# A two-block transformer kernel: the condition's broadcast loaded by stride-zero transfers, two small sums and one turn placed earlier

## The chip, the cores and the metric

The kernel runs on one core of a Trainium2 chip. A core has TensorE (PE, matrix products, with its weight loads shown as PEld), VectorE (DVE), ScalarE (ACT), GpSimd (POOL) and SyncE (SP), which here only issues transfers. The engines run their own instruction queues in order and wait for one another through semaphores. The metric is the device time of one execution in microseconds (us), lower is better. The time of a kernel is the median of its runs.

## The reference

A transformer block with two token streams (512 tokens of x, 256 of ctx, width 1024) is followed by a second block. What matters here stands at the start of the first: a condition vector c makes shifts, scales and gates for x (`adaln_params`), another, c_ctx, makes them for ctx; both streams are normed, modulated and projected by `w_in`. Lambda is one scalar of the attention.

```python
def rmsnorm(x, g):
    xf = x.astype(jnp.float32)
    y = xf * lax.rsqrt(jnp.mean(xf * xf, axis=-1, keepdims=True) + EPS)
    return (y * g.astype(jnp.float32)).astype(x.dtype)

def modulate(x, g, shift, scale):
    return rmsnorm(x, g) * (1 + scale) + shift

def adaln_params(cond, w_mod, b_mod):
    return jnp.split(jax.nn.silu(cond) @ w_mod + b_mod, 6, axis=-1)
...
        lam = (jnp.exp(jnp.sum(diff_lambda_q[l, 0] * diff_lambda_k[l, 0]))
               - jnp.exp(jnp.sum(diff_lambda_q[l, 1] * diff_lambda_k[l, 1])) + lam_init)
        sh1, sc1, gt1, sh2, sc2, gt2 = [m[:, None, :] for m in adaln_params(c, w_mod[l], b_mod[l])]
        csh1, csc1, cgt1, csh2, csc2, cgt2 = adaln_params(c_ctx, w_mod[l], b_mod[l])
        pc = project(modulate(ctx, norm1_g[l], csh1, csc1), w_in[l])
...
        px = project(modulate(x, norm1_g[l], sh1, sc1), w_in[l])
...
        x = x + gt1 * mix
        x = x + gt2 * swiglu(modulate(x, norm2_g[l], sh2, sc2), w_ffn_in[l], w_ffn_out[l])
```

All arithmetic is float32. The second block (pooling, attention, memory attention, a convolved feed-forward) is untouched.

## The kernel before

Activations lie with the 1024 features on the partitions, as eight tiles (k = 0 to 7) of 128 x 512 for x and 128 x 256 for ctx. A product with weights is made of three passes: each operand is split into a high part (`whi`, `hxh`, `hch`) and a rest (`wlo`, `hxl`, `hcl`), and TensorE adds high by high, high by rest and rest by high. Weights come in units of up to 128 x 1024 (`raw`, ring of four, loaded by SyncE in the order of a plan); ScalarE's `hi(upto)` makes `whi` (ring of three), `lo(upto)` on VectorE makes `wlo` (for units 1 and 2 GpSimd does). SyncE loads unit j when the rest of unit j - 4 has been made. Every engine's code is one hand-written sequence; there is no scheduler, and the order on an engine is the order of the lines.

The start of the program runs so:

- Transfers. ScalarE issues c and c_ctx as two rows (`crow`), `ident` and `vec`. SyncE issues, in this order on one queue, the modulation weights `mod1` pieces 0 to 3 (0.5 MB each), ctx (`cmT`), x (`xT`), pieces 4 to 15 with `raw` units 0 to 3 between and behind them, the constants, and `raw` 4 and on.
- TensorE turns the condition into columns (L2159), which ScalarE passes through Silu (`small`, semaphore `cb`). Then two products of a row of ones with a row of c (L2177, one partition deep) spread c over 128 partitions in banks 6 and 7, from where ScalarE's Silu puts it into `cbx` (L605).
- `mod_piece(n)` (L2188) multiplies the two condition columns with piece n: four matmul records each, pieces 0 to 7 for the first half of the features and 8 to 15 for the second. ScalarE copies the two result rows of a half out (`mod_rows`, `mrow`), `turn_mods(half)` (L2166) turns them back into columns, VectorE's `first_mods` adds the bias and makes the gains.
- `first_sums` (L2173) sums squares over the partitions for ctx (bank 4) and x (bank 5): ScalarE squares, VectorE adds, TensorE multiplies with ones. `root` on ScalarE and `newton` on VectorE make the reciprocal root. A like product of two columns makes the sums of lambda in bank 3 (L2201), of which ScalarE takes the exponential (L622) inside its loop over the split (i = 6).
- The loop i = 0 to 15 makes the normed tiles, x and ctx in turn: `first_norm` on VectorE (L1298), the high part on ScalarE (L629), `first_rest` on VectorE (L1305). i = 8 to 15 need the second half of the modulations.
- TensorE's first projection, "gqk", has eight steps k (L2238 to L2240 for x, into banks 0 to 3; L2246 to L2248 for ctx, into banks 4 and 5), 18 products each. Pieces 12 to 15 stand between steps 1 and 2, `turn_mods(1)` after step 2. A bank is written only when the semaphores in `freed[b]` have been reached; `fill(b)` waits for them.

The gates and the second pair of shift and scale need the rest of `w_mod`. They are not made on TensorE: its rows are loaded transposed (`mraw`), and `dots2` on VectorE multiplies each with the spread condition and sums, with `cbx` for rows 0 to 15 and `cbx2` from row 16. `cbx2` is made anew since its place is used by others between: ScalarE loads c again (`crow2`, L872) during the attention, TensorE spreads it by two one-row products into banks 4 and 5 (L2483) ahead of the output projection "wo", ScalarE applies Silu (L903). In "wo" each of the eight units m has 24 products (L2112 to L2114).

## Time and profile before

| | |
|---|---|
| median of three runs | 1660.71 us (1660.3 to 1662.28) |
| the profiled execution | 1659.81 us, its span 1658.2 us |
| TensorE busy | 1582.9 us, 95% of the span |
| VectorE busy | 938.3 us, 57% |
| ScalarE busy | 730.5 us, 44% |
| GpSimd busy | 125.1 us, 8% |
| transfers | 156.60 MB, mean 94 GB/s |

The profile is of one execution. "Busy" counts instructions that run; matmuls are pipelined, so a start and a length may overlap with the next. In a timeline a row has its start, its length and, in brackets, how long the engine stood idle before it and what released it; the first rows of the program lie within the first 75 us. Starts are counted from the span's start.

### The profile page before, as it was taken

How to read it: one execution, taken by the hardware profiler on the slowest of the kernel's cores; microseconds unless marked ns; L12 is line 12 of the kernel's file. 1: busy time of each engine (PE TensorE's matmuls, PEld its weight loads, DVE VectorE, ACT ScalarE, POOL GpSimd, SP SyncE). 2: the span in 40 equal slices, each digit the busy share in tenths (PEclk: the TensorE clock that was granted, in tenths of full speed). 3: DMA queues.
4: the chain of work that ended last, by engine and by line, in shares of the span. 5: the costliest groups of instructions: out<-in, count | busy, mean ns of one | idle time of the engine just before them, and what ended most of it. 6: DMA issues, size and time to landing. Idle time of an engine off the chain costs nothing.

```text
span 1658.2 us, 19178 instructions
## 1 busy us (share of the span) xinstructions
PE 1582.9 (95%) x7606; PEld 1245.1 (75%) x7606; DVE 938.3 (57%) x1441; ACT 730.5 (44%) x1130; POOL 125.1 (8%) x89
## 2 busy tenths in 40 slices
PE   7999999899899999999999899999987999999999
PEld 2677876677688888888878677788665788888885
DVE  4476787885844433334555555366656586257743
ACT  4344445675332222323342767455455444234432
POOL 0000123531000000000010011130010000000000
PEclk9999999699999999999999999999988999999999
DMA  9351111101534233222332222143202232333221
GB/s 376 130 188 52 50 50 54 64 1 66 176 114 147 75 108 106 100 78 88 102 102 70 63 69 74 44 142 106 78 24 91 64 115 70 108 114 92 83 89 54
DMA packets 47950, 156.60 MB, mean 94 GB/s; under 512 B 5587, under 2 KB 10323, under 8 KB 47350
## 3 DMA queue, kind: packets, MB, share of 16 engines
q1 hardware_dynamic: 47280, 152.00, 27.8%
q10 hardware_dynamic: 582, 3.38, 0.6%
q8 instruction: 61, 1.00, 0.2%
q14 instruction: 27, 0.22, 0.0%
HBM read 153.26 MB, written 2.10 MB: 94 GB/s over the span
## 4 chain that ended last, share of the span: by engine, by line
PE 79%; DVE 11%; ACT 6%; issue 3%; DMA 0%; POOL 0%; ACTq 0%; DVEq 0%
PE pall L2112 19%; PE pall L2113 18%; PE pall L2114 18%; PE pall L2605 2%; PE pall L2188 1%; PE pall L2130 1%; PE pall L2132 1%; PE pall L2131 1%; PE pall L2148 1%; PE pall L2607 1%; PE pall L2606 1%; PE pall L2149 1%; PE pall L2150 1%; DVE wlo L1243 1%; ACT whi L563 1%
## 5 line engine op out<-in xcount | busy, mean ns | idle before, releaser
L1243 DVE TENSOR_TENSOR wlo<-raw,whi 128x1024 fp32r<-128x1024 f32 (+2 forms) x261 | 290.6, 1115 | 313.5 <-ACT whi L563 313.3
L563 ACT ACTIVATE whi<-raw 128x1024 fp32r<-128x1024 f32 (+2 forms) x263 | 247.0, 941 | 208.9 <-PE pall L2114 177.3
L2112 PE MATMUL pall<-h5h,whi 128*128 128x512 f32 x320 | 125.8, 393 | 2.5 <-DVE wlo L1243 2.5
L2113 PE MATMUL pall<-h5l,whi 128*128 128x512 f32 x320 | 125.3, 392 | 0.0
L2114 PE MATMUL pall<-h5h,wlo 128*128 128x512 f32 x320 | 125.2, 391 | 0.0
L2112 PE MATMUL pall<-h2h,whi 128*128 128x512 f32 x320 | 124.6, 389 | 0.0
L2114 PE MATMUL pall<-h2h,wlo 128*128 128x512 f32 x320 | 124.6, 389 | 0.0
L2113 PE MATMUL pall<-h2l,whi 128*128 128x512 f32 x320 | 124.6, 389 | 0.0
L2112 PEld LDWEIGHTS pall<-h5h,whi 128*128 128x128 f32 x320 | 60.4, 189 | 15.7 <-issue 3.1
L2114 PEld LDWEIGHTS pall<-h5h,wlo 128*128 128x128 f32 x320 | 60.5, 189 | 12.7
L2113 PEld LDWEIGHTS pall<-h5l,whi 128*128 128x128 f32 x320 | 60.5, 189 | 12.6 <-issue 0.2
L2112 PEld LDWEIGHTS pall<-h2h,whi 128*128 128x128 f32 x320 | 60.1, 188 | 12.5
L2114 PEld LDWEIGHTS pall<-h2h,wlo 128*128 128x128 f32 x320 | 60.1, 188 | 12.5
L2113 PEld LDWEIGHTS pall<-h2l,whi 128*128 128x128 f32 x320 | 60.1, 188 | 12.3
L2113 PE MATMUL pall<-cl,whi 128*128 128x512 f32 x176 | 68.6, 390 | 0.0
L2114 PE MATMUL pall<-ch,wlo 128*128 128x512 f32 x176 | 68.6, 390 | 0.0
L2112 PE MATMUL pall<-fh,whi 128*128 128x512 f32 x176 | 68.5, 389 | 0.0
L2112 PE MATMUL pall<-ch,whi 128*128 128x512 f32 x176 | 68.5, 389 | 0.0
L2113 PE MATMUL pall<-fl,whi 128*128 128x512 f32 x176 | 68.5, 389 | 0.0
L2114 PE MATMUL pall<-fh,wlo 128*128 128x512 f32 x176 | 68.5, 389 | 0.0
L945 ACT ACTIVATE fh<-tmp 128x512 fp32r<-128x512 f32 x22 | 13.9, 632 | 95.1 <-DVE tmp L1695 95.1
L1912 DVE TENSOR_TENSOR pall<-pall,R 128x512 f32<-128x512 f32 x48 | 33.1, 695 | 35.2 <-PE pall L2114 31.2
(459 smaller groups left out, 3653.7 us busy)
## 6 DMA issues: line engine op xcount, KB each, us to landing
raw<-in_weights SPq DMA_DIRECT2D x204, 512.0 KB, 3.5
mraw<-in_wmod SPq DMA_DIRECT2D x32, 512.0 KB, 5.1
mod<-in_weights SPq DMA_DIRECT2D x16, 512.0 KB, 15.2
raw<-in_weights SPq DMA_DIRECT2D x25, 256.0 KB, 2.6
raw<-in_weights SPq DMA_DIRECT2D x32, 192.0 KB, 2.3
xT<-in_x SPq DMA_DIRECT2D x1, 2048.0 KB, 13.1
xT<-in_x ACTq DMA_DIRECT2D x1, 2048.0 KB, 8.2
out_y<-xT SPq DMA_DIRECT2D x8, 256.0 KB, 2.1
```

The source lines that it names most:

```text
L563: e.activation(whi[j % 3][:, 0:cols(j)], raw[j % 4][:, 0:cols(j)], ACT.Copy).then_inc(s.hi, 1)
L1243: e.tensor_tensor(wlo[j % 3][:, 0:n], raw[j % 4][:, 0:n], f(whi[j % 3][:, 0:n]), ALU.subtract).then_inc(s.lo_v, 1)
L1912: e.tensor_tensor(bank(b), bank(b), r, ALU.mult).then_inc(s.rq, 1)
L2112: e.matmul(o_, a[:, kk, :], xh(k), start=(k == 0), stop=False)
L2113: e.matmul(o_, a[:, kk, :], xl(k), start=False, stop=False)
L2114: mm = e.matmul(o_, b[:, kk, :], xh(k), start=False, stop=(k == nk - 1))
L2130: e.matmul(bank(o_), a[:, k % 2, c], xh(k), start=(k == 0), stop=False)
L2131: e.matmul(bank(o_), a[:, k % 2, c], xl(k), start=False, stop=False)
L2132: mm = e.matmul(bank(o_), b[:, k % 2, c], xh(k), start=False, stop=(k == 7))
L2148: e.matmul(bank(o_), h_, a[:, kk, :], start=(k + kk == 0), stop=False)
L2149: e.matmul(bank(o_), h_, b[:, kk, :], start=False, stop=False)
L2605: e.matmul(bank(b), a[:, k, :], xh[:, k, :], start=(k == 0), stop=False)
```

## The change

1. `cbx` is no longer made by products of one row: SyncE loads c into all 128 partitions by one transfer whose source has a stride of zero (128 x 1024 values, 0.5 MB written), after `raw` 3 and before the constants. ScalarE applies Silu in place, one instruction of 128 x 1024, at i = 8 of its split loop ahead of `mod_rows(1)`; this needs the Silu table and then the exponential's again.
2. `cbx2` is loaded in the same way by ScalarE's queue at n = 19 of the attention loop; `crow2` and the products of L2483 go.
3. The context sum stands after piece 3 instead of 5, lambda's sums behind it instead of after piece 11, the token sum after piece 7 instead of behind the first turn. Lambda's exponential stands behind the context root. On ScalarE `root("x")` stands before `hi(0)`.
4. `lo(0)` on VectorE stands inside the loop, behind the first `first_rest`.
5. `turn_mods(1)` stands inside step 2, after two of its four x groups.

The diff, with its declarations left out:

```diff
@@ SyncE
             for j in range(2, 4):
                 load(j)
+            e.dma_start(cbx[:, :], ap["cc"][:, 0, :].to_broadcast([128, 1024])).then_inc(s.cc, 16)
             for dst, name in consts:
@@ ScalarE
-            for j in range(2):
-                w.wait_ge(s.p_cb, 2 + j)
-                e.activation(cbx[:, 512 * j:512 * j + 512], bank(6 + j), ACT.Silu).then_inc(s.cb, 1)
             for q in range(16):
...
             root("ctx", bank(4, 256), 256, D)
+            w.wait_ge(s.lam_p, 1)
+            e.activation(small[:, 4:6], bank(3, 2), ACT.Exp).then_inc(s.lam_a, 1)
             mod_rows(0)
+            root("x", bank(5), 512, D)
             hi(0)
-            root("x", bank(5), 512, D)
             for i in range(16):
-                if i == 6:
-                    w.wait_ge(s.lam_p, 1)
-                    e.activation(small[:, 4:6], bank(3, 2), ACT.Exp).then_inc(s.lam_a, 1)
                 if i == 8:
+                    w.wait_ge(s.cc, 48)
+                    e.activation(cbx[:, :], cbx[:, :], ACT.Silu).then_inc(s.cb, 1)
+                    table[0] = "silu"
+                    use_exp()
                     mod_rows(1)
...
-                if n == 5:
-                    e.dma_start(crow2[0:1, :], ap["cc"][:, 0, :]).then_inc(s.cc, 16)
+                if n == 19:
+                    e.dma_start(cbx2[:, :], ap["cc"][:, 0, :].to_broadcast([128, 1024])).then_inc(s.cc, 16)
...
             w.wait_ge(s.kql, 8)
-            for j in range(2):
-                w.wait_ge(s.p_cb, 4 + j)
-                e.activation(cbx2[:, 512 * j:512 * j + 512], bank(4 + j), ACT.Silu).then_inc(s.cb, 1)
+            w.wait_ge(s.cc, 64)
+            e.activation(cbx2[:, :], cbx2[:, :], ACT.Silu).then_inc(s.cb, 1)
             table[0] = "silu"
             use_exp()
@@ VectorE
             first_mods(0)
-            lo(0)
             newton("x", bank(5), 512, D)
             for i in range(16):
...
                 if i and i != 8:
                     first_rest(i - 1)
+                if i == 1:
+                    lo(0)
@@ TensorE
-            w.wait_ge(s.g_const, 2)
-            for j in range(2):
-                e.matmul(bank(6 + j), ones[0:1, :], crow[0:1, 512 * j:512 * j + 512], start=True, stop=True).then_inc(s.p_cb, 1)
-                freed[6 + j] = [(s.cb, 2 + j)]
             w.wait_ge(s.cb, 1)
...
             for n in range(9):
                 mod_piece(n)
-                if n == 5:
+                if n == 3:
                     first_sums(4, 256, 7, acc_c)
+                    w.wait_ge(s.lam_v, 1)
+                    fill(3)
+                    e.matmul(bank(3, 2), ones[:, :], small[:, 2:4], start=True, stop=True).then_inc(s.lam_p, 1)
+                    freed[3] = [(s.lam_a, 1)]
+                if n == 7:
+                    first_sums(5, 512, 14, acc)
             turn_mods(0)
-            first_sums(5, 512, 14, acc)
             for n in range(9, 12):
                 mod_piece(n)
-            w.wait_ge(s.lam_v, 1)
-            fill(3)
-            e.matmul(bank(3, 2), ones[:, :], small[:, 2:4], start=True, stop=True).then_inc(s.lam_p, 1)
-            freed[3] = [(s.lam_a, 1)]
...
                 for i in range(4):
+                    if k == 2 and i == 2:
+                        turn_mods(1)
+                        freed[6] = [(s.mdv, 4)]
+                        freed[7] = [(s.mdr, 4)]
...
-                if k == 2:
-                    turn_mods(1)
-                    freed[6] = [(s.mdv, 4)]
-                    freed[7] = [(s.mdr, 4)]
...
-            w.wait_ge(s.cc, 48)
-            for j in range(2):
-                fill(4 + j)
-                e.matmul(bank(4 + j), ones[0:1, :], crow2[0:1, 512 * j:512 * j + 512], start=True, stop=True).then_inc(s.p_cb, 1)
-                freed[4 + j] = [(s.cb, 4 + j)]
```

TensorE before, between piece 5 and the first step (`acc_c` and `acc` are the summed squares of ctx and x, `small` the columns of lambda, `mrow` the rows that are turned):

```order
L2188 MATMUL pall<-mod_5,small 2x512 x2
L2173 MATMUL pall<-acc_c,ones 128x256
L2188 MATMUL pall<-mod_6,small 2x512 x2
L2188 MATMUL pall<-mod_7,small 2x512 x2
L2188 MATMUL pall<-mod_8,small 2x512 x2
L2166 MATMUL pall<-ident,mrow 128x2 x8
L2173 MATMUL pall<-acc,ones 128x512
L2188 MATMUL pall<-mod_9,small 2x512 x2
L2188 MATMUL pall<-mod_10,small 2x512 x2
L2188 MATMUL pall<-mod_11,small 2x512 x2
L2201 MATMUL pall<-small,ones 128x2
L2238 MATMUL pall<-hxh,whi 128x512
```

TensorE in the changed kernel, from piece 3 to piece 9:

```order
L2183 MATMUL pall<-mod_3,small 2x512 x2
L2172 MATMUL pall<-acc_c,ones 128x256
L2192 MATMUL pall<-small,ones 128x2
L2183 MATMUL pall<-mod_4,small 2x512 x2
L2183 MATMUL pall<-mod_5,small 2x512 x2
L2183 MATMUL pall<-mod_6,small 2x512 x2
L2183 MATMUL pall<-mod_7,small 2x512 x2
L2172 MATMUL pall<-acc,ones 128x512
L2183 MATMUL pall<-mod_8,small 2x512 x2
L2165 MATMUL pall<-ident,mrow 128x2 x8
L2183 MATMUL pall<-mod_9,small 2x512 x2
```

All three small products have moved ahead, and the token sum now comes before the turn.

ScalarE in the split loop, from the fifth tile of x's and ctx's first half to `mod_rows(1)`, as a difference (`cbx` is the spread condition):

```order
-L622 ACTIVATE small<-pall 128x2
 L629 ACTIVATE hxh<-tmp,modv 128x512
 L629 ACTIVATE hch<-tmp,modv 128x256
 L563 ACTIVATE whi<-raw 128x1024
+L621 ACT_TABLE_LOAD
+L621 ACTIVATE cbx<-cbx 128x1024
+L556 ACT_TABLE_LOAD
 L601 ACTIVATE mrow<-pall 2x512 x2
 L629 ACTIVATE hxh<-tmp,modv 128x512
```

The exponential has left the loop, and a Silu between two table loads stands ahead of the second half's rows.

VectorE in the changed kernel, from the last modulations of the first half to the second tile of x:

```order
L1287 SCALAR_TENSOR_TENSOR gsv<-modv,vec 128x4 x2
L1253 SCALAR_TENSOR_TENSOR W<-pall,W 128x512
L1255 SCALAR_TENSOR_TENSOR R<-W,R 128x512
L1297 SCALAR_TENSOR_TENSOR tmp<-xT,gsv,R 128x512
L1297 SCALAR_TENSOR_TENSOR tmp<-cmT,gsv,R 128x256
L1304 SCALAR_TENSOR_TENSOR hxl<-tmp,modv,hxh 128x512
L1242 TENSOR_TENSOR wlo<-raw,whi 128x1024
L1297 SCALAR_TENSOR_TENSOR tmp<-xT,gsv,R 128x512
```

Before, the same stretch read:

```order
L1288 SCALAR_TENSOR_TENSOR gsv<-modv,vec 128x4 x2
L1243 TENSOR_TENSOR wlo<-raw,whi 128x1024
L1254 SCALAR_TENSOR_TENSOR W<-pall,W 128x512
L1256 SCALAR_TENSOR_TENSOR R<-W,R 128x512
L1298 SCALAR_TENSOR_TENSOR tmp<-xT,gsv,R 128x512
L1298 SCALAR_TENSOR_TENSOR tmp<-cmT,gsv,R 128x256
L1305 SCALAR_TENSOR_TENSOR hxl<-tmp,modv,hxh 128x512
```

The split of unit 0 has moved from ahead of Newton's step to behind the first `hxl`.

## Rows read from the trace of the kernel before

**Rows 1.** The page's chain that ended last, by engine.

```profile
PE 79%; DVE 11%; ACT 6%; issue 3%; DMA 0%; POOL 0%; ACTq 0%; DVEq 0%
```

**Rows 2.** TensorE's timeline: start, length (us), line, operands, idle before and its releaser.

```profile
7.00 3.76 PE L2177 MATMUL pall<-crow,ones 1*128 1x512 f32 x4
10.69 12.09 PE L2188 MATMUL pall<-mod,small 128*2 128x512 f32 x24
22.70 0.70 PE L2173 MATMUL pall<-acc_c,ones 128*128 128x256 f32 x2
...
29.15 1.13 PE L2173 MATMUL pall<-acc,ones 128*128 128x512 f32 x2
30.21 5.31 PE L2188 MATMUL pall<-mod,small 128*2 128x512 f32 x12
...
36.34 0.47 PE L2238 MATMUL pall<-hxh,whi 128*128 128x512 f32 x1 [0.51 <-DVE hxl L1305]
...
42.60 0.80 PE L2238 MATMUL pall<-hxh,whi 128*128 128x512 f32 x1 [3.94 <-ACT small L622]
...
50.19 7.03 PE L2188 MATMUL pall<-mod,small 128*2 128x512 f32 x16
...
73.08 0.50 PE L2238 MATMUL pall<-hxh,whi 128*128 128x512 f32 x1 [1.05 <-DVE wlo L1243]
```

**Rows 3.** Windows: stretch, length, each engine's busy us, granted clock, transfer share, GB/s.

```profile
20.00:30.00 10.00, 10.00 (x31) 2.52 (x29) 4.28 (x11) 5.28 (x9) 0.00 (x0) 1.00 1.03 409
42.00:43.00 1.00, 0.40 (x1) 0.40 (x2) 1.00 (x2) 0.55 (x2) 0.00 (x0) 0.50 0.36 74
48.00:49.00 1.00, 1.00 (x6) 0.83 (x5) 0.00 (x0) 0.00 (x0) 0.88 (x2) 0.94 0.00 0
300.00:320.00 20.00, 15.39 (x50) 11.29 (x50) 16.83 (x29) 11.12 (x21) 9.65 (x7) 0.52 0.24 96
```

**Rows 4.** VectorE's timeline, same columns, in the first 75 us.

```profile
17.60 5.47 DVE L1276 TENSOR_TENSOR acc<-acc,tmp 128x512 f32<-128x512 f32 x7 [1.72 <-ACT tmp L613]
...
32.36 0.69 DVE L1254 SCALAR_TENSOR_TENSOR W<-pall,W 128x512 f32<-128x512 f32 x1 [1.33 <-ACT W L579]
...
33.91 0.75 DVE L1298 SCALAR_TENSOR_TENSOR tmp<-xT,gsv,R 128x512 f32<-128x512 f32 x1
...
61.49 0.24 DVE L1285 TENSOR_TENSOR modv<-pall,vec 128x8 f32<-128x8 f32 x2 [16.28 <-PE pall L2166]
```

**Rows 5.** ScalarE's timeline, same columns.

```profile
16.42 0.63 ACT L613 ACTIVATE acc<-xT 128x512 f32<-128x512 f32 x1 [2.21 <-DMA xT<-in_x]
...
57.26 0.59 ACT L601 ACTIVATE mrow<-pall 2x512 f32<-2x512 f32 x1 [11.23 <-PE pall L2188]
...
399.65 1.28 ACT L903 ACT_TABLE_LOAD   x1
400.95 1.09 ACT L903 ACTIVATE cbx<-pall 128x512 f32<-128x512 f32 x2
```

**Rows 6.** TensorE and VectorE at the output projection, same columns.

```profile
394.62 2.18 PE L2483 MATMUL pall<-crow,ones 1*128 1x512 f32 x4
396.72 0.80 PE L2112 MATMUL pall<-mixh,whi 128*128 128x512 f32 x1
...
414.55 0.39 PE L2112 MATMUL pall<-mixh,whi 128*128 128x512 f32 x1
...
410.48 1.23 DVE L1328 CUSTOM_DVE_ANT_0 mraw<-mraw,cbx 128x1024 f32<-128x1024 f32 x1 [4.05 <-DMA mraw<-in_wmod]
...
411.63 1.23 DVE L1243 TENSOR_TENSOR wlo<-raw,whi 128x1024 fp32r<-128x1024 f32 x1
```

**Rows 7.** Weight loads of the pieces, same columns.

```profile
13.20 0.13 PEld L2188 LDWEIGHTS pall<-mod,small 128*2 128x2 f32 x1 [0.72 <-issue]
14.03 0.09 PEld L2188 LDWEIGHTS pall<-mod,small 128*2 128x2 f32 x1 [0.69 <-issue]
14.46 0.09 PEld L2188 LDWEIGHTS pall<-mod,small 128*2 128x2 f32 x1 [0.34 <-issue]
```

4 lines of the change are left out of this document (1 added, 3 removed).

## The prediction

> **What bounds the kernel now.** I read four views in this order. The chain of waits gives TensorE 79% of the path that sets the end [rows 1], so the question for each edit is what it moves on TensorE or what TensorE waits for. TensorE's timeline of the first 75 us [rows 2] shows how the first projection starts: products of the modulation weights (64 records, 16 pieces of four), sums, and then steps k = 0 to 7 of the projection. Three things are lost there: the one-row products of L2177 ahead of the pieces; a stall of 3.94 us in step 0, released by ScalarE's exponential of lambda, because the fourth matmul group needs bank 3, which holds lambda's sums; and 1.05 us before step 6. The windows [rows 3] show what follows the stall: a granted clock of 0.50 (1.2 GHz) at 42 to 43 us and a return to 2.4 GHz in 48 to 49. VectorE's timeline [rows 4] shows what releases the steps, ScalarE's [rows 5] how long that engine waits for the last pieces. The second site is at 394 us [rows 6].
>
> **Start of the pieces.** The products of L2177 go (four records). The pieces begin behind the transposes and the small Silu, at about 7.4 instead of 10.69 us [rows 2]. Their weight loads are 0.83 us apart up to 14.03 and 0.43 us from there [rows 7]. TensorE ran at half speed first, though the granted clock reads 1.00. The rise came 3.35 us after the first 128-row product; the one-row products before it, 3.7 us of them, had not brought it. I take the same for the new order: piece 0 slow until 10.75, and pieces 1 to 3 at 1.72 us each (5.31 us for three, [rows 2]) to 15.9. The other bound is a rise at 14.03 as before, pieces 0 and 1 both slow.
>
> **Sums.** The context sum (0.7 us, [rows 2]) follows piece 3; lambda's has two columns and costs less. That is at most 17.3; the context adds end before VectorE turns to xT at 17.60. Now data binds: xT landed at 16.4 [rows 5], and piece 4 is the next 0.52 MB of the same queue at 409 GB/s [rows 3], 1.28 us, so 17.7. Pieces 4 to 7 take 6.9 us, to 24.6; their data lands every 1.28 us, faster than they are used. The token sum (1.06 us, 30.21 less 29.15) needs VectorE's adds, over at 23.07 [rows 4]; it ends at 25.6, not 30.2. Piece 8, to 27.35, and the turn (0.6) to 27.95.
>
> **The chain to step 0.** Modulations 28.0 to 28.55. ScalarE's root of the token sum took until 32.36, 2.15 us after the sum's end at 30.21 [rows 2, 4]; now it is done at 27.8, earlier than the modulations. So VectorE goes on with Newton (1.55 us, 32.36 to 33.91), first norm at 30.1. Step 0 began 2.43 us after that norm (33.91 to 36.34), released by hxl: 32.5. The moved `lo(0)` comes behind hxl: 1.2 us, as the split in [rows 6], to 33.7. It is paid on the path, where before it lay in ScalarE's root time, and the next norms stand behind it. TensorE has pieces 9 to 11 until 33.15, so 0.6 us of it is covered by these. Step 0 starts at **33.7** instead of 36.34: 2.6 us.
>
> **Steps 0 to 5.** Lambda's exponential now comes on ScalarE right behind the context root, ten microseconds before TensorE wants bank 3. The 3.94 us stall ends. What is late next is VectorE: behind `lo(0)` a norm of 0.75 us and hcl, half as wide and by an estimate from that norm 0.5 us, ready at 34.9 and wanted after the twelve token products, 2.9 us after the start at 36.6; then a norm and hxl, 36.1, wanted at 37.3. Steps 2 to 5 with the turn took 14.8 us (57.22 to 72.03, [rows 2]), so a step is (14.8 - 0.6) / 4 = 3.55 us and steps 0 and 1 cost 7.1 instead of 13.85 us (36.34 to 50.19). These 6.75 us are the stall and 2.8 us of half clock; I let the clock stay up, since nothing else in the first 36 us brought it down. So: 33.7 + 7.1 = 40.8, pieces 12 to 15 (7.0) to 47.8.
>
> **Second half of the modulations.** ScalarE must have made mrow before the turn, which now stands two matmul groups (6 of a step's 15 product lengths, 1.4 us) into step 2, at 49.2. Before, it fell idle at 46.03 (57.26 less 11.23, [rows 5]) and nothing but 0.59 us of mrow lay between that and its split, so it is free at 46.03 - 0.59 - 2.6 = 42.8. There it now waits for cbx, a transfer put on SyncE's queue behind 16 others of 0.52 MB that follow xT: 17 x 1.28 = 21.8 us after 16.4, landed at 38.2. It delays the constants and raw 4 by 1.28 us each, which are wanted after 60 us. A table load, a Silu of 128x1024 and a load back: 1.28 + 1.09 + 1.28 = 3.65 us [rows 5], to 46.4, mrow's first row at 47.0; the second waits for piece 15 and ends at 48.4, 0.8 us ahead of the turn. Taken at nothing: the cover is the wait for the pieces (11.23 us in the row). The turn gives modulations at 49.8 rather than 61.49 [rows 4]. Step 6 began 11.59 us after them (73.08), held by the split of the fourth unit; that is now 61.4. TensorE itself gets there at 47.8 + 14.8 = **62.6** instead of 73.08; the 1.05 us stall is gone with 1.2 us to spare. **First site: 10.5 us.** The transfers of mraw wait for norms that come 11.7 us earlier, so they shift with it.
>
> In the Trainium skill (ScalarE: Activation LUTs, What ACT_TABLE_LOAD costs) a switch costs about 2.66 us, 1.28 for the load and the rest for a drain. By that the two switches (5.3 us) end mrow at 50.4 and the turn is 1.2 us late: an estimate of 1649.8. Here the Silu begins 0.02 us after its load's end [rows 5], so the row decides for 1.28.
>
> **The second site.** The products of L2483 go: the output projection starts at 394.6 instead of 396.72, 2.1 us [rows 6]. The broadcast is issued by ScalarE in an idle stretch at about 390.5 and has 10 us to land. ScalarE's chain stays (one Silu for two, 0.05 us). So wlo for unit 3 of this projection stays where it was, at 412.86, behind a row product that waits for mraw until 410.48 [rows 6]. TensorE reached unit 3 at 414.55; 2.1 us earlier is 412.45, and it would wait 0.4. **Gain 1.65 us**, whether or not the clock still falls there. If it stays up, TensorE only waits longer for the same wlo.
>
> **Sum.** 10.5 + 1.65 = 12.1 us. The profiled execution took 1659.81 (span 1658.2), 0.9 under the median of 1660.71. So 1647.7 for such an execution, and **1648.6** for the median. Between the two sites nothing is bound by an absolute time: transfers there are released by engines that shift too.
>
> **Rivals.** (a) *Clock rises no sooner*: it rises at 14.03 with pieces 0 and 1 slow. For it: the clock is the chip's, not the queue's. Against it: the row of one-row products. Price: piece 2 begins at 14.1, piece 3 ends at 17.5, the sums at 18.6, 0.9 us behind: 1649.5. (b) *Half clock without a stall*: the first step starts behind a gap and falls to 1.2 GHz as in [rows 3], 2.8 us: 1651.4. (c) *Later stalls meet another clock*: everything behind shifts by 10 us, and the projection's neighbourhood at 300 to 320 us runs at 0.52 [rows 3]. One stretch like that of 41 to 48 us costs 3.3 us more or less: 1651.9 or 1645.3. (d) *The slower side: the broadcasts run on one of 16 transfer engines*. No row shows a transfer with source stride zero. On 16 engines it takes 1.28 us, on one 16 times that, 20.5 us. It decides from a landing later than 43.6 us (42.8 plus the 0.8 us of cover). Begun at 36.9 it would land at 57.4, mrow at 62.2, the turn 13 us late: the first site loses 2.5. The second lands at 411, its Silu, load and split and wlo end at 415.6 where unit 2 was begun at 409.1 (one unit, 5.44 us or 24 products, ahead of unit 3 in [rows 6]): 6.5 us more. About +9: 1670. Against it: the destination has 128 rows of 4 KB, as raw has. (e) *It does nothing measurable*: the early gain is eaten by a wait for weights after step 7: 1660.
>
> The Trainium skill (DMA: Bandwidth & Descriptors, Rules for kernel authors) says that a leading stride-zero dimension of fewer than 16 copies confines a transfer to that many engines; here the leading dimension is 128 copies, so by it all 16 work and (d) does not come. No run yet shows it.
>
> **Chances.** Forecast 62%, (a) 10%, (b) 10%, (c) upward 6%, downward 4%, (d) 5%, (e) 3%. A measurement of this kernel tells about 0.2% (3.3 us) from no change. Faster: all but (d) and (e), 0.92; same 0.03; slower 0.05. The range from 1645 takes in (c) downward; to 1653.5 it takes in (a), (b), (c) upward and 1.6 us of spread such as the runs before show (1660.3 to 1662.28). Outside are (d), (e) and the tails.
>
> **What would show it.** Right: TensorE's first piece at 7.4; records 0.43 us apart from about 10.7; step 0 at 33.7 and no row with a wait for `small` in it; granted clock 1.00 from 40 to 48; ScalarE's Silu with one table load on either side ending before 46.5; step 6 at 62 to 63 with no wait over 0.2 us; the output projection started 2 us sooner behind the last head's sum, with a new wait for wlo of 0.3 to 1 us at its unit 3. Wrong: a wait for cbx on ScalarE, or one for mrow on TensorE in step 2; a clock of 0.50 between 34 and 48; a stall before unit 2 of the output projection; or a difference that appears only after 100 us.

## The result and the profile after

The changed kernel took a median of 1650.4 us (four runs, 1647.16 to 1652.87) against 1660.51 us (four runs, 1660.18 to 1662.28) of the kernel before in the same measurement: a ratio of 0.9936, with a 95% interval of 0.9917 to 0.9955. The gain, 10.1 us or 0.6%, lies clear of the 0.2% that a measurement tells from no change. The forecast was 1648.6 us and a range of 1645.0 to 1653.5. The profiled execution took 1650.24 us, its span 1648.4 against 1658.2 before.

TensorE's timeline of the changed kernel shows the first stretch; its rows answer to [rows 2].

```profile
7.31 8.67 PE L2183 MATMUL pall<-mod,small 128*2 128x512 f32 x16 [0.27 <-ACT small L595]
16.00 0.70 PE L2172 MATMUL pall<-acc_c,ones 128*128 128x256 f32 x2
...
17.79 7.03 PE L2183 MATMUL pall<-mod,small 128*2 128x512 f32 x16 [0.98 <-DMA mod<-in_weights]
24.75 1.12 PE L2172 MATMUL pall<-acc,ones 128*128 128x512 f32 x2
...
27.62 0.66 PE L2165 MATMUL pall<-ident,mrow 2*128 2x2 f32 x8
...
33.87 0.50 PE L2238 MATMUL pall<-hxh,whi 128*128 128x512 f32 x1 [0.35 <-DVE wlo L1242]
...
40.98 7.03 PE L2183 MATMUL pall<-mod,small 128*2 128x512 f32 x16
...
49.53 0.65 PE L2165 MATMUL pall<-ident,mrow 2*128 2x2 f32 x8
```

Three losses of before are gone. The row products are not there, so the pieces begin at 7.31 instead of 10.69. Between step 0 (33.87) and piece 12 (40.98) lie 7.11 us where there were 13.85: the row with 3.94 us of waiting for `small` has no successor, and the clock does not fall. The last product of step 5 starts at 62.61 and step 6 follows at 62.73 without a wait, where before step 6 started at 73.08 behind one of 1.05 us. What stands new in the brackets is small: 0.98 us for piece 4's data and 0.35 us for `wlo`.

The window over the end of step 1 and pieces 12 to 15 has a granted clock (the third figure from the end) of 1.00, against the 0.50 at 42 to 43 in [rows 3]:

```profile
41.00:48.00 7.00, 7.00 (x18) 1.32 (x17) 1.88 (x4) 6.37 (x7) 3.23 (x2) 1.00 0.57 189
```

ScalarE's timeline shows the new Silu with a table load on either side, and the two rows of `mrow`; the engine comes to the first load at 43.24, straight from the split of a weight unit, and has no wait for the transfer of c in front of the Silu. VectorE's has the first norm and the moved `lo(0)`.

```profile
42.19 1.04 ACT L563 ACTIVATE whi<-raw 128x1024 fp32r<-128x1024 f32 x1
43.24 1.28 ACT L621 ACT_TABLE_LOAD   x1
44.54 1.06 ACT L621 ACTIVATE cbx<-cbx 128x1024 f32<-128x1024 f32 x1
45.61 1.28 ACT L556 ACT_TABLE_LOAD   x1
46.91 0.59 ACT L601 ACTIVATE mrow<-pall 2x512 f32<-2x512 f32 x1
48.04 0.59 ACT L601 ACTIVATE mrow<-pall 2x512 f32<-2x512 f32 x1 [0.55 <-PE pall L2183]
```

```profile
28.31 0.24 DVE L1284 TENSOR_TENSOR modv<-pall,vec 128x8 f32<-128x8 f32 x2 [3.95 <-PE pall L2165]
...
30.39 0.75 DVE L1297 SCALAR_TENSOR_TENSOR tmp<-xT,gsv,R 128x512 f32<-128x512 f32 x1
...
32.59 1.22 DVE L1242 TENSOR_TENSOR wlo<-raw,whi 128x1024 fp32r<-128x1024 f32 x1
...
50.22 0.24 DVE L1284 TENSOR_TENSOR modv<-pall,vec 128x8 f32<-128x8 f32 x2 [7.34 <-PE pall L2165]
```

At the second site TensorE's rows show units 0 and 3 of the output projection, both now behind a short wait. VectorE's show why unit 3 waits: a row product of `mraw`, itself behind its transfer, stands ahead of the unit's `wlo`, as in [rows 6].

```profile
383.87 0.79 PE L2111 MATMUL pall<-mixh,whi 128*128 128x512 f32 x1
...
390.17 0.50 PE L2111 MATMUL pall<-mixh,whi 128*128 128x512 f32 x1 [0.97 <-DVE mixl L1604]
...
402.62 0.50 PE L2111 MATMUL pall<-mixh,whi 128*128 128x512 f32 x1 [0.60 <-DVE wlo L1242]
```

```profile
400.19 1.23 DVE L1327 CUSTOM_DVE_ANT_0 mraw<-mraw,cbx 128x1024 f32<-128x1024 f32 x1 [4.04 <-DMA mraw<-in_wmod]
401.35 1.22 DVE L1242 TENSOR_TENSOR wlo<-raw,whi 128x1024 fp32r<-128x1024 f32 x1
```

To see where the gain is at a given point of the program, I take instructions of ScalarE that stand in both kernels (roots of norms, mostly) and subtract their starts. This shift, in us earlier than in the profile of before, is used for every experiment; the head of a column is the instruction's time before.

| | 313.6 | 367.2 | 394.7 | 444.6 | 818.7 | 1105.0 | 1641.2 |
|---|---|---|---|---|---|---|---|
| after | 10.40 | 10.24 | 10.26 | 11.79 | 11.01 | 9.75 | 9.95 |

The start gives 10.42 (at 192.0 us), of which 10.26 are left at the last head's root (394.7). The second site adds 1.67 up to unit 3: together 11.93. Two stretches behind it give some back. The feed-forward starts with TensorE at half clock. Before, it began at 450.48 and the clock was back at about 454.1, 3.6 us on; now it begins at 438.68 and the clock is back at about 444.1, 5.4 us on. At half clock 1.8 us more cost 0.9 by this reckoning; the table's step from 444.6 to 818.7 is 0.78. And at 922 us the clock falls behind a wait for `merged`, which costs 1.25 us by the rows on either side; the profile of before has no fall there. TensorE's row and the windows (granted clock third from the end):

```profile
443.00:444.00 1.00, 1.00 (x4) 0.72 (x3) 1.00 (x3) 0.72 (x1) 0.00 (x0) 0.50 0.00 0
444.00:445.00 1.00, 1.00 (x6) 0.84 (x5) 1.00 (x2) 0.42 (x1) 0.00 (x0) 0.93 0.00 0
922.00:926.00 4.00, 3.50 (x9) 2.83 (x10) 1.04 (x2) 1.61 (x3) 0.00 (x0) 0.57 0.11 23
```

```profile
922.50 0.77 PE L2595 MATMUL pall<-pmh,whi 128*128 128x512 f32 x1 [2.64 <-DVE merged L1789]
```

### The profile page after: what moved, and what is told of

Read it like the earlier page. It is cut to its first block, busy times and chain, and to the rows that moved or that the text cites. A ratio compares the mean times of both kernels' runs of the same rounds, so it can differ in the third digit from the quotient of the medians.

```text
span 1648.4 us, 19160 instructions
## 1 busy us (share of the span) xinstructions
PE 1575.0 (96%) x7598; PEld 1241.1 (75%) x7598; DVE 938.2 (57%) x1441; ACT 733.2 (44%) x1130; POOL 125.1 (8%) x89
## 4 chain that ended last, share of the span: by engine, by line
PE 79%; DVE 10%; ACT 7%; issue 3%; DMA 1%; POOL 0%; SPq 0%; ACTq 0%; DVEq 0%
PE pall L2111 18%; PE pall L2112 18%; PE pall L2113 18%; PE pall L2595 2%; PE pall L2129 1%; PE pall L2131 1%; PE pall L2130 1%; PE pall L2147 1%; PE pall L2596 1%; PE pall L2597 1%; PE pall L2149 1%; PE pall L2148 1%; DVE wlo L1242 1%; PE pall L2183 1%; ACT whi L563 1%
## 6 DMA issues: line engine op xcount, KB each, us to landing
raw<-in_weights SPq DMA_DIRECT2D x32, 192.0 KB, 2.3
```

## The experiments

Each kernel is the changed one with the edit shown, unless it says otherwise. "Before" beside a run was measured on the same chip. With one run each, a total tells little here: the changed kernel's own runs spread over 5.7 us. The rows decide.

### The changed kernel again, without an edit

> The changed kernel, unaltered, profiled once more. In its first profile 12.0 us were gained by unit 3 of the output projection and 2.2 us of them lost again: 0.9 us where the clock came back 5.4 us after the feed-forward's first product (3.6 us in the kernel before), and 1.2 us near 923 us, where it fell after a wait. Theory: where the clock falls and rises is a matter of the execution, not of the kernel, so this profile has step 6 of the first projection at 62.5 to 63.0 us and the output projection's unit 3 at 402.6 us again, within 0.2 us, while the shift against the kernel before at the end of the span differs from 9.8 us by over 0.5 us, and the stretch of half clock at the feed-forward has another length. Rival: the loss belongs to the new alignment of the kernel's own work; then both stretches come back with the same lengths and the span is 1648.4 within 0.3 us.

It took 1649.11 us (before beside it: 1660.75), and from step 0 to step 6 its lengths are those of after (28.86 us in both). The rival, that both losses come back with the same lengths, did not come. But the theory missed too: step 6 was at 63.35 and unit 3 at 404.11, later than I allowed. Two stretches differed, and both by the clock. TensorE's first pieces, and the weight loads with the change of rhythm:

```profile
7.25 9.85 PE L2183 MATMUL pall<-mod,small 128*2 128x512 f32 x16 [0.27 <-ACT small L595]
```

```profile
12.32 0.13 PEld L2183 LDWEIGHTS pall<-mod,small 128*2 128x2 f32 x1 [0.73 <-issue]
13.07 0.09 PEld L2183 LDWEIGHTS pall<-mod,small 128*2 128x2 f32 x1 [0.62 <-issue]
```

The loads come 0.43 us apart only from 13.07 (the next is at 13.50), that is 5.82 us after the first 128-row product; in the profile of after it was 10.67 (3.36 us). Step 0 started at 34.49, 0.6 us later. The other place is 354 to 358 us, where this execution had a fall of the clock and after's had its own earlier, at 341 to 349; the shift at 394.7 is 8.89 instead of 10.26. Both were given back: half clock lasted 6.8 us at the feed-forward (10.2 in after), and at 917.5 us the clock fell ahead of the wait for `merged` instead of behind it. That wait then took 1.04 us instead of 2.64 and covered the loss. So the end stands at 11.08, better than after's 9.95.

### Lambda's exponential back in its old place

```diff
             root("ctx", bank(4, 256), 256, D)
-            w.wait_ge(s.lam_p, 1)
-            e.activation(small[:, 4:6], bank(3, 2), ACT.Exp).then_inc(s.lam_a, 1)
...
             for i in range(16):
+                if i == 6:
+                    w.wait_ge(s.lam_p, 1)
+                    e.activation(small[:, 4:6], bank(3, 2), ACT.Exp).then_inc(s.lam_a, 1)
```

> The changed kernel with one thing undone: ScalarE takes lambda's exponential inside the split loop at i = 6, as before, while the sums stay early on TensorE. Theory: bank 3 is held until then, so TensorE stands in step 0 behind its third group, from about 36.2 to 40.3 us (4 us), and half clock follows; the steps behind come 4 to 7 us later (3.9 for the stall, up to 2.9 for the clock), and the total is 1654 to 1657 us. Rival: VectorE's norms were late anyway, so step 0 only swaps its releaser and the loss is under 1.5 us.

1658.78 us (before 1660.75). TensorE's row of the stall, and the window over it:

```profile
40.45 0.73 PE L2239 MATMUL pall<-hxh,whi 128*128 128x512 f32 x1 [4.02 <-ACT small L619]
```

```profile
40.00:44.00 4.00, 3.55 (x12) 3.07 (x13) 3.06 (x6) 3.15 (x6) 0.52 (x1) 0.57 0.95 334
```

Stall and half clock are back together. From step 0 (34.10) to piece 12 (47.08) are 12.98 us against 7.11: 5.87, of which 4.02 is the wait and 1.85 the clock. The shift is 4.35 at 313.6 us instead of 10.40. So this one instruction's place is worth 5.9 us, over half of the whole gain, and the fall of the clock came with the stall and not with the start of the step. The product that makes its sums stayed early in this run; no run puts that back. The total is higher than I expected because 3 us more went at 928 to 935 us, where this execution ran 6.8 us at half clock.

### What the one-row products did: two tests

Two products are put ahead of the pieces again, and nothing reads them. In the first they are one row deep, as in the kernel before:

```diff
+            w.wait_ge(s.g_const, 2)
+            for j in range(2):
+                e.matmul(bank(6 + j), ones[0:1, :], crow[0:1, 512 * j:512 * j + 512], start=True, stop=True)
```

> The changed kernel with the two one-row products put back ahead of the pieces, into banks 6 and 7, read by nobody. Theory: one-row products do not bring the clock up. The pieces start at 10.7 us, their records stand 0.85 us apart until about 14.1 us, piece 3 ends at 19.3 us, and step 0 starts 2.4 us later than the 33.87 us of the changed kernel; total 1652.5 us. Rival: the clock rises by time from TensorE's first work, whatever that is; then the rise is at 10.7 us too, piece 3 ends at 17.7 us and step 0 starts at most 0.9 us late.

In the second they are 128 rows deep, with the same number of columns:

```diff
+            w.wait_ge(s.g_const, 2)
+            for j in range(2):
+                e.matmul(bank(6 + j).rearrange("p (a n) -> p a n", a=4), ones[:, :],
+                         ones[:, :].unsqueeze(1).to_broadcast([128, 4, 128]), start=True, stop=True)
```

> As the kernel with the two one-row products ahead of the pieces, but the products are 128 rows deep (ones by ones), of the same number and width. Theory: these count, so the clock rises near 10.7 us as in the changed kernel although no piece has run by then; pieces start at 10.7 us and stand 0.43 us apart from the first, piece 3 ends at 17.6 us and step 0 starts 0.5 to 0.9 us later than 33.87 us. Rival: it is the pieces themselves or their data that decide; then this kernel does as the one with one-row products, records 0.85 us apart until 14.1 us and step 0 2.4 us late.

The first took 1651.63 us, the second 1650.02 (before 1660.75). TensorE's timelines, the first kernel's and then the second's:

```profile
6.94 3.76 PE L2176 MATMUL pall<-crow,ones 1*128 1x512 f32 x4
10.62 9.42 PE L2186 MATMUL pall<-mod,small 128*2 128x512 f32 x16
```

```profile
7.62 3.52 PE L2176 MATMUL pall<-ones 128*128 128x512 f32 x4
11.07 7.03 PE L2187 MATMUL pall<-mod,small 128*2 128x512 f32 x16
```

Nearly the same time goes into the four records. Behind 128-row products the sixteen pieces' records all run at 2.4 GHz (7.03 us, as at 40.98 in after); behind one-row products they need 9.42. The first kernel's weight loads:

```profile
14.84 0.13 PEld L2186 LDWEIGHTS pall<-mod,small 128*2 128x2 f32 x1 [0.72 <-issue]
15.59 0.09 PEld L2186 LDWEIGHTS pall<-mod,small 128*2 128x2 f32 x1 [0.62 <-issue]
```

The clock rises at 15.59: 8.65 us after the first one-row product, but 4.97 us after the first 128-row one. Step 0 starts at 36.80, 2.93 us behind after (2.4 expected), and in the second kernel at 34.86, 0.99 behind, 0.3 of it since the products waited for `ones`. That the one-row products had done nothing for the clock was the ground on which the prediction's start stood, and it held. In the three profiles that have them ahead of the pieces the rise came 7.03, 7.91 and 8.65 us after the first of them, later than any delay in the list below.

The first kernel also shows what the rest of the new order is worth at step 0. It has the sums, the roots and `lo(0)` in their new places, and starts step 0 at 36.80, no sooner than before (36.34, and 36.80 in its second profile). Its clock rose later, though: at 15.59 against 14.03 and 14.80. If a later rise costs half of its delay, the kernel before would have come to 37.1 or 37.2 with it. So by this estimate the new order gained 0.3 to 0.4 us at step 0, and nearly all of the 2.47 us there are the products.

How soon the rise comes after the first 128-row product is another matter. It is read from the first weight load whose successor comes sooner, so to within about half a microsecond. In the order of the delay, over the twelve profiles with a visible rise, before among them: 3.29 (`lo(0)` ahead, below), 3.34 (before), 3.36 (after), 4.22 (before again), 4.91, 4.97, 4.97, 4.99, 5.08, 5.82, 5.85, 5.93 us. The 3.35 that I took from one execution lies at the lower end.

### The turn back behind step 2

```diff
-                    if k == 2 and i == 2:
-                        turn_mods(1)
-                        freed[6] = [(s.mdv, 4)]
-                        freed[7] = [(s.mdr, 4)]
+                if k == 2:
+                    turn_mods(1)
+                    freed[6] = [(s.mdv, 4)]
+                    freed[7] = [(s.mdr, 4)]
```

> The changed kernel with the second turn behind step 2 again. Theory: the turn moves from 49.5 to 51.5 us, the modulations by 1.95 us, and the split of the fourth unit that step 6 needs, ready 1.1 us early now, comes 0.8 us late: step 6 waits 0.7 to 1.0 us and all behind shifts by that. Rival: the earlier turn only gave slack, since the pieces came early enough: then no wait at step 6 and under 0.2 us.

1651.94 us (before, nine runs: 1660.42). The wait ahead of step 6 is back, as in the last of [rows 2]:

```profile
64.01 0.50 PE L2234 MATMUL pall<-hxh,whi 128*128 128x512 f32 x1 [0.98 <-DVE wlo L1242]
```

The shift is 9.11 at 313.6 us, 1.3 less than after's: 0.98 by this wait, 0.17 by a later step 0. The turn inside the step is worth 1.0 us.

### `lo(0)` ahead of Newton's step

```diff
+            lo(0)
             newton("x", bank(5), 512, D)
...
-                if i == 1:
-                    lo(0)
```

> The changed kernel with the split of unit 0 on VectorE ahead of Newton's step again. Theory: it is paid on the path in both places: the first norm comes 1.2 us later and hxl at 33.9 instead of 32.6 us (on the first profile's times), so step 0 begins 5.65 to 5.8 us after the first modulations instead of 5.56, 0.1 to 0.2 us later, and step 6 likewise. Rival: moving it was worth the whole 1.2 us, since before it waited for ScalarE's copy as well; then step 0 begins 6.5 us or more after the modulations.

1652.68 us (before, nine runs: 1661.35). TensorE's row at step 0:

```profile
33.90 0.47 PE L2237 MATMUL pall<-hxh,whi 128*128 128x512 f32 x1 [0.58 <-DVE hxl L1304]
```

Step 0 starts 5.78 us after the modulations (28.12) and 5.56 us after them (28.31) in after: the place of the 1.22 us instruction is worth 0.22. Either way it lies on VectorE's path to step 0. The higher total has nothing to do with it, since the shift is 10.53 at 313.6 and 10.34 at 394.7, a little better than after's; it comes from 6.8 us of half clock at 921 to 929.

### The slower side: a broadcast that one transfer engine carries

```diff
-            e.dma_start(cbx[:, :], ap["cc"][:, 0, :].to_broadcast([128, 1024])).then_inc(s.cc, 16)
+            e.dma_start(cbx[0:127, :], ap["cc"][:, 0, :].to_broadcast([127, 1024])).then_inc(s.cc, 16)
+            e.dma_start(cbx[127:128, :], ap["cc"][:, 0, :]).then_inc(s.cc, 16)
```

and the same for `cbx2`, with the waits raised to match, so that rival (d) of the prediction is made to happen.

> The changed kernel with both stride-zero transfers cut into 127 rows and 1 row. If the number of transfer engines follows the number of rows, 127 rows go through one engine. Theory: then each takes about 20 us instead of 1.3: ScalarE waits for the first until 55 to 60 us instead of not at all, the turn comes 11 to 14 us late and the gain of the first site (10.4 us) is gone; the second lands about 20 us after 379 us plus that shift, ScalarE waits for it 8 to 10 us, and unit 2 of the output projection waits 4 to 8 us; total 1660 to 1672 us, slower than or equal to the kernel before. Rival: 127 rows are spread over all engines as 128 are, and nothing moves by over 0.5 us.

1679.31 us (before 1660.42), above the expected 1660 to 1672. ScalarE's row at the first Silu and TensorE's at the turn, then ScalarE at the second site:

```profile
59.65 1.06 ACT L622 ACTIVATE cbx<-cbx 128x1024 f32<-128x1024 f32 x1 [15.25 <-DMA cbx<-in_cc]
```

```profile
63.13 1.01 PE L2167 MATMUL pall<-ident,mrow 2*128 2x2 f32 x8 [13.67 <-ACT mrow L602]
```

```profile
402.64 0.60 ACT L883 ACTIVATE tmp<-pall 128x512 f32<-128x512 f32 x1 [6.87 <-issue]
...
416.65 1.28 ACT L904 ACT_TABLE_LOAD   x1 [5.60 <-DMA cbx<-in_cc]
```

A view of the transfers alone, for 400 to 420 us in 40 slices of half a microsecond, gives the rate of the one engine:

```profile
GB/s 25 33 25 25 25 33 25 25 25 25 66 25 25 25 33 25 25 25 25 33 25 25 25 25 33 25 25 25 25 25 33 25 0 0 0 0 0 0 0 0
```

The issue of the last row, behind that of 127 rows, on SyncE and on ScalarE:

```profile
23.54 18.98 SPq L529 DMA_DIRECT2D cbx<-in_cc  x1
```

```profile
394.82 7.72 ACTq L874 DMA_DIRECT2D cbx<-in_cc  x1
```

The mechanism is the one of rival (d): the Silu waits for the transfer, the turn is 13.6 us late (49.53 to 63.13). The first site ends 4.92 us slower than before and not 2.5. TensorE's clock fell during that wait, at 53.6 us, and came back at 67.2. Only the 4.1 us behind the turn had work in them: from the turn to step 3 are 4.58 us against 2.78 in after, a loss of 1.8. The second site costs 6.1 and then 7.7 us, more than the 6.5 in all that (d) had. The reason is one that I had not priced. The engine that issued the transfer was held at its next issue, SyncE for 18.98 us and ScalarE for 7.72. The 6.87 us of "issue" in ScalarE's row above are these, and the 6.1 us are lost across them. So (d) would have come out near 1679 and not 1670. In the changed kernel itself nothing of this is seen: `cbx2` is issued by ScalarE at 379.00 and the data moves from 380 to 382.2 us, at up to 451 GB/s; ScalarE comes to `cbx` at 43.24 and does not wait. The rate is the measured difference between 128 copies and 127. The Trainium skill (DMA: Bandwidth & Descriptors, Why a DMA increments its semaphore by 16 and not by 1) has the number of engines as the largest one, up to 16, that divides the leading size of both sides, and so one engine for 127 and 16 for 128: the runs agree (25 to 33 against up to 451 GB/s).

### The second site by products again

```diff
-            w.wait_ge(s.cc, 64)
-            e.activation(cbx2[:, :], cbx2[:, :], ACT.Silu).then_inc(s.cb, 1)
+            for j in range(2):
+                w.wait_ge(s.p_cb, 2 + j)
+                e.activation(cbx2[:, 512 * j:512 * j + 512], bank(4 + j), ACT.Silu).then_inc(s.cb, 1)
@@ TensorE
...
+            for j in range(2):
+                fill(4 + j)
+                e.matmul(bank(4 + j), ones[0:1, :], crow2[0:1, 512 * j:512 * j + 512], start=True, stop=True).then_inc(s.p_cb, 1)
...
```

(with the load of `crow2` in place of that of `cbx2`).

> The changed kernel with the second site undone: the condition is loaded as one row and spread by two one-row products ahead of the output projection, as before. Theory: the output projection starts 2.1 us or more later behind the last head's sum, but its unit 3 only 1.6 to 1.7 us later (404.2 instead of 402.6 us with the same first site), since in the changed kernel that unit waits 0.5 to 0.9 us for a split that VectorE makes at 402.5 us in both; total 1.65 us over the changed kernel's. Rival: the split is not what binds there; then the full 2.1 to 2.9 us of the start stay to unit 3 and beyond.

1649.42 us (before 1660.42). TensorE's rows at the products and at unit 3, and the window behind the products:

```profile
385.18 1.98 PE L2481 MATMUL pall<-crow,ones 1*128 1x512 f32 x4
...
403.54 0.49 PE L2113 MATMUL pall<-mixh,whi 128*128 128x512 f32 x1
```

```profile
387.00:388.00 1.00, 1.00 (x5) 0.78 (x5) 0.68 (x1) 0.29 (x1) 0.00 (x0) 1.00 0.00 0
```

The distance from the root of the last head (385.28) to unit 3 is 18.26 us. It is 18.15 in after and 19.82 in the profile of before. So with the products back the site lost 0.1 us and not the 1.65 expected. Even that is within the spread: the seven profiles of kernels that load `cbx2` as the changed kernel does, with the rows of `w_mod` where it has them, have 18.15 to 18.36. The 2 us of products were covered, nearly whole, by the two waits that stand in after's rows, 0.97 for `mixl` and 0.60 for `wlo`; neither stands in this run's. What before lost here it lost to the clock, which this time did not fall.

### The kernel before again, without an edit

> The kernel before the change, unaltered, profiled once more. In its first profile TensorE had half clock for 3.4 us at the start of the output projection (396 to 400 us), and the projection's unit 3 began 19.8 us after the last head's root. In the kernel with the second site undone the clock stayed up there and unit 3 began 18.26 us after the root, as early as with the broadcast by transfer (18.15). Theory: that fall is a matter of the execution, and the second site's gain of 1.67 us was measured against an unlucky profile; then in this one the clock may stay up, and if it does unit 3 begins at 18.2 to 18.4 us. Rival: the kernel before always falls there; then 19.8 us again. The stall of 3.9 us and 6.8 us of half clock at the first step are in the kernel either way (3.4 to 6.8 us of half clock).

1660.74 us, beside nine runs with a median of 1661.35. The window behind its second pair of one-row products:

```profile
397.00:398.00 1.00, 1.00 (x3) 0.44 (x2) 0.29 (x1) 0.64 (x2) 0.00 (x0) 0.66 0.00 0
```

The clock falls there as in the first profile (half clock at 397 to 401), and unit 3 is 19.83 us behind the root, against 19.82. The stall of step 0 is the same 3.94 us. So the theory, that the clock may stay up, was wrong and the rival came: the fall is there in both executions of the kernel before.

### The rows of `w_mod` a unit sooner

The 4.04 us that VectorE waits for `mraw` ahead of `wlo` come from the plan, which loads rows 16 to 19 of `w_mod` behind unit 6 of the projection.

```diff
-        DOT_LOADS = {6: (0, 4), 7: (4, 8), 8: (8, 12), 9: (12, 16), J["wo", 6, 0]: (16, 20), J["wo", 7, 0]: (20, 21)}
+        DOT_LOADS = {6: (0, 4), 7: (4, 8), 8: (8, 12), 9: (12, 16), J["wo", 5, 0]: (16, 20), J["wo", 7, 0]: (20, 21)}
```

> The changed kernel, and SyncE issues the four weight rows 16 to 19 for VectorE's sums behind unit 5 of the output projection's weights instead of behind unit 6, so they no longer wait for unit 2's split. Theory: VectorE's product at 400.2 us waits no more (4.0 us), the split of unit 3 is ready by 399.5 us, and unit 3 starts at 401.7 instead of 402.6 us: 0.9 us gained, all of it kept, ratio to the kernel before 0.9927. Rival: the DMAs of the rows then stand in front of unit 6's weights and delay that split; or TensorE is held by the first head's split (0.97 us at 390.2) alone and nothing is gained.

In five rounds 1647.81 us (1647.08 to 1648.29), a ratio of 0.9921 (0.9907 to 0.9934) to the kernel before. VectorE's rows:

```profile
396.20 1.22 DVE L1327 CUSTOM_DVE_ANT_0 mraw<-mraw,cbx 128x1024 f32<-128x1024 f32 x1
...
397.94 1.23 DVE L1242 TENSOR_TENSOR wlo<-raw,whi 128x1024 fp32r<-128x1024 f32 x1 [0.51 <-ACT whi L563]
```

The wait is gone, and unit 3 starts 17.42 us behind the root (384.60 to 402.02) without one, 0.73 us less than in after. This is the best version found. Its interval overlaps with after's (0.9917 to 0.9955), so the chip's medians alone do not separate the two; the 0.73 us is by the rows.

### Sooner rows, and the second site by products

The last edit and that of the second site together: with no wait for `wlo` left, do the products cost their 2 us?

> The kernel with the weight rows issued sooner, with the second site undone (one row loaded, spread by two one-row products). Theory: the broadcast by transfer was worth nothing at unit 3 because of the split that VectorE made behind its wait for rows; with that wait gone TensorE itself binds, so now the products cost something: unit 3 begins 18.26 us after the last head's root instead of 17.42, 0.84 us later; of the 2.4 us that the start moves the rest goes into the wait for the last head's split (0.94 us) and fewer microseconds of overlap. Rival: another wait takes the place of the first and both stay at 17.4.

1651.43 us (before, nine runs: 1661.35). TensorE started the products at 385.13 and ran at half clock from 387.8 on for 3.4 us, as this window within it shows.

```profile
388.00:389.00 1.00, 1.00 (x4) 0.81 (x3) 0.96 (x2) 0.00 (x0) 0.00 (x0) 0.50 0.00 0
```

Unit 3 came 19.87 us behind the root, 2.45 more than with the sooner rows alone, where 0.84 was expected. By an estimate the products took 0.84 of it (18.26, with products and a full clock, less 17.42) and the clock 1.6, near the half of 3.4 us. With this the clock fell behind one-row products at this place in 3 of 4 profiles (before, before again, this one; not in the one with the second site by products), and in none of the nine that have no products and no held engine there. That is a strong habit and no law, and why one execution escaped is open. No run has products of 128 rows at this place, so it is not shown that their depth brings the fall here.

### Sooner rows, dummy products at the start, units 0 and 1 side by side

Three 128-row products of ones are put at the very start, to have the clock up when the pieces begin, and units 0 and 1 of the output projection run their steps 0 to 6 each before either runs step 7, which waits for the last head.

```diff
+            for j in range(3):
+                e.matmul(bank(6).rearrange("p (a n) -> p a n", a=4), ones[:, :],
+                         ones[:, :].unsqueeze(1).to_broadcast([128, 4, 128]), start=True, stop=True)
...
-            for m in range(8):
+            for ks in (range(7), (7,)):
+                for (ua, ub), m in pair:
...
+            for m in range(2, 8):
```

> The kernel with the weight rows issued sooner, and two more edits. One: three products of ones by ones (128 rows deep, 512 wide, read by nobody) run from 1 to about 6 us, before the condition has landed. Theory: the clock is up when the pieces begin, all records 0.43 us apart; TensorE then waits for piece 4's data until 17.7 to 17.8 us in every execution, where it began it at 17.8 to 18.8 us; 0 to 0.6 us. Two: in the output projection units 0 and 1 both run their steps 0 to 6 first and step 7 afterwards, so the last head's split is not waited for: unit 3 begins 16.5 us after the last head's root instead of 17.42. Together 0.9 to 1.5 us under the kernel with the rows sooner: 1646.6, ratio to the kernel before 0.9915. Rival for two: unit 0's result comes 5 us later, the splits of units 3 and 4 wait for it, and TensorE stands there instead.

In five rounds 1650.34 us (1646.16 to 1650.72), a ratio of 0.9924 (0.991 to 0.9937): 1646.6 was expected, and missed. TensorE's rows of the start, and a window:

```profile
1.00 4.49 PE L2158 MATMUL pall<-ones 128*128 128x512 f32 x6 [1.00 <-POOL ones L2014]
...
6.83 7.03 PE L2187 MATMUL pall<-mod,small 128*2 128x512 f32 x16 [0.27 <-ACT small L595]
...
16.11 0.70 PE L2176 MATMUL pall<-acc_c,ones 128*128 128x256 f32 x2 [2.26 <-DVE acc_c L1275]
...
17.91 8.72 PE L2187 MATMUL pall<-mod,small 128*2 128x512 f32 x16 [0.98 <-DMA mod<-in_weights]
```

```profile
18.00:22.00 4.00, 4.00 (x6) 0.59 (x5) 3.48 (x6) 3.98 (x7) 0.00 (x0) 0.57 1.03 411
```

The first pieces were all fast, and then TensorE had nothing: it waited 2.26 us for the context's sum of squares and 0.98 for piece 4, the clock fell at 18 us, and step 0 came at 35.68, 1.8 us later than in after. Speed ahead of a bound that data sets had bought a stall. The second half of the edit did what it should: unit 3 is 16.67 us behind the root instead of 17.42.

The shifts of the experiments, as in the table above:

| | 313.6 | 367.2 | 394.7 | 444.6 | 818.7 | 1105.0 | 1641.2 |
|---|---|---|---|---|---|---|---|
| after again | 9.84 | 8.87 | 8.89 | 10.31 | 10.74 | 10.78 | 11.08 |
| one-row products at the start | 7.49 | 6.53 | 6.53 | 7.92 | 8.30 | 8.40 | 8.58 |
| 128-row products at the start | 9.44 | 9.88 | 8.83 | 10.24 | 10.13 | 10.30 | 10.17 |
| turn behind step 2 | 9.11 | 8.69 | 8.71 | 10.19 | 9.35 | 7.92 | 8.25 |
| `lo(0)` ahead | 10.53 | 10.33 | 10.34 | 11.68 | 10.94 | 8.12 | 7.49 |
| rows sooner | 10.43 | 11.14 | 10.13 | 12.54 | 12.34 | 12.37 | 12.20 |
| sooner rows and products | 10.45 | 9.49 | 9.50 | 9.46 | 8.93 | 8.97 | 8.71 |
| sooner rows, dummies, pair | 8.62 | 9.32 | 8.23 | 11.39 | 10.51 | 9.22 | 9.47 |

What differs in a row from 313.6 to 394.7 and from 818.7 on, in code that no edit touched, is the clock: some of the stretches at half speed lie elsewhere in each execution. A stretch whose loss a later wait covers costs little, as at 917.5 us in the second execution. Over the whole span they add up to 75 us in both profiles of before, which have the same stretches 1 us apart, to 92 us in the kernel with the slow broadcast, and to 61 to 75 us in the others.

## Why the prediction was right, and where it was off

- **Start of the pieces.** Right: 7.4 forecast, 7.31 measured; rise 10.75 against 10.67; end of piece 3 at 15.9 against 15.98. That it fell so close was partly luck. That one-row products do nothing for the clock at the start is shown by the pair of tests; the delay of 3.35 us had one execution behind it, and of the twelve delays in the profiles, before's among them, three are like it and nine are 4.2 to 5.9. With 5.8, as in the second execution, rival (a) was half true: 0.6 us later at step 0, where (a) said 0.9.
- **Sums.** Right: piece 4 at 17.7 against 17.79, held by its data; pieces 4 to 7 to 24.6 against 24.75; the turn from 27.35 against 27.62.
- **The chain to step 0.** Right: modulations 28.0 against 28.31, norm 30.1 against 30.39, step 0 at 33.7 against 33.87, held by `lo(0)` as said. The 0.3 us at the turn were made up where the rest of the chain took a little less than before.
- **Steps 0 to 5.** Right, and the largest term: 7.1 forecast, 7.11 measured. The test with the exponential back in the loop gives 5.9 us for it, 4.0 of stall and 1.85 of half clock. The other 0.9 is that half clock lasted 6.8 us in before and 3.4 in the test. Rival (b), a fall without a stall, did not come: the windows from 33 to 63 us read 1.00 in all ten profiles with the exponential early and the broadcast on 16 engines.
- **Second half of the modulations.** Right: ScalarE free at 42.8 against 43.24, no wait for `cbx`, `mrow` at 46.91, turn at 49.2 against 49.53, modulations 49.8 against 50.22, step 6 at 62.6 against 62.73, without a wait. Here the first load begins 0.01 us behind the split ahead of it (42.19 + 1.04 to 43.24), the Silu 0.02 us behind the end of the load (43.24 + 1.28 to 44.54), and the load back and the copy behind it follow as closely. So the rows decide for 1.28 us a switch. The 2.66 us of the Trainium skill (ScalarE: Activation LUTs, What ACT_TABLE_LOAD costs) is not what a load adds on this path.
- **First site.** 10.5 forecast, 10.42 measured: 2.47 to step 0, 6.74 in steps 0 and 1, 1.05 at step 6, 0.16 in the rest.
- **The second site.** The number was right (1.65 against 1.67 at unit 3), the account of it half wrong. I wrote that the gain came whether or not the clock fell. The wait for `wlo` at unit 3 came as forecast (0.4, measured 0.60), but a second one of 0.97 us at step 7 of unit 0, for the last head's `mixl`, stands in no line of the prediction. Together they eat the 2.1 us of products almost whole: with products and a clock that stayed up unit 3 came 0.1 us later than in after. The prediction names the fall there and gives it no part in the gain. Three of the four profiles with products fell to half clock, and only these lost. So what the edit bought is mostly a fall that no longer comes. That the forecast came out was luck: the two bounds (2.1 less the wait; the fall) happened to be near each other.
- **Sum.** 12.1 forecast; 11.93 at unit 3 and 9.95 at the end. What failed is the sentence that nothing between the sites and behind them is bound by an absolute time. The rows show no transfer that was; but the stretches at half clock did not shift with the program. 0.8 to 0.9 us at the feed-forward and 1.25 at 922 us are the upward side of rival (c), which I had priced and left out of the sum. The profiled execution came out 2.5 us above the 1647.7 forecast for it, and the median 1.8 us above 1648.6.
- **Range.** The allowance of 1.6 us for spread was taken from runs of before. The changed kernel's four runs spread over 5.7 us where before's beside them spread over 2.1 (and another nine of before over 4.0). Its median lies inside 1645.0 to 1653.5; a single run might as well have been 1647 or 1653.
- **Rival (d).** It did not come in the changed kernel. Made to happen, it gave 1679.3 where I had 1670; of the 9 us more, 6.1 are the shift up to the root at 394.7, with ScalarE's queue held, and 2.4 come at the first site, 1.8 of them by half clock.

## What to carry over

A small instruction whose result frees a bank is worth what stands behind it: moving one exponential of two columns, with its sums made early enough, gave 5.9 of 10 us, and what showed it was the wait in brackets ahead of a matmul, not a busy share. When an edit takes work off TensorE, look for the waits of every engine that this work covered before you book its length, and don't speed TensorE up ahead of a bound that data sets, since the idle time behind it can cost the clock. Broadcast a row with all 128 partitions as the leading dimension: at 127 it is another transfer.

## What the runs showed of the chip that I had not expected

- Products of one row left the clock low at the start (in the test it rose 8.65 us after the first of them, and 4.97 us after the first product of 128 rows), and it fell behind them at 387 to 401 us in three of four profiles.
- The same program's clock rose 3.36 or 5.82 us after its first 128-row product, and some of its later stretches at half clock lay elsewhere in the second execution. Its two profiled executions differ by 1.1 us. The fastest and the slowest of its runs, 5.7 us apart, have mean granted clocks of 0.982 and 0.978, but no profile; that the clock alone spread them is not shown. The Trainium skill (TensorE: Matmul & The Clock Gate, What's actually happening) calls the number of slow matmuls at the start variable between runs, and the rows agree.
- A transfer of 127 rows with source stride zero runs at 25 to 33 GB/s, and the engine that issued it stands at its next issue for 7.7 us (ScalarE) and 19.0 us (SyncE).
